# Four experts instead of three in 64-slot fp32 steps, and a new order of the 32 expert steps

## The reference

```
def moe_ffn(x, w_router, wg, wu, wd):
    B, S, D = x.shape
    xt = x.reshape(B * S, D)
    logits = (xt @ w_router).astype(jnp.float32)
    top_v, top_i = lax.top_k(logits, TOP_K)
    w = jax.nn.softmax(top_v, axis=-1)
    gates = jnp.sum(jax.nn.one_hot(top_i, N_EXPERTS, dtype=jnp.float32) * w[..., None], axis=1)
    y = jnp.zeros_like(xt)
    for e in range(N_EXPERTS):
        y = y + gates[:, e:e + 1].astype(xt.dtype) * swiglu(xt, wg[e], wu[e], wd[e])
    return y.reshape(B, S, D)
```

## Time and profile before

| | |
|---|---|
| median of 3 runs | 1435.05 us (1435.01 to 1440.6) |
| the profiled execution's own time | 1436.74 us |
| its span, from the first to the last instruction | 1435.0 us |
| TensorE busy, share of the span | 97% |
| VectorE, ScalarE busy | 57%, 49% |
| weights and other data moved | 444.37 MB |
| mean granted TensorE clock | 0.986 of full |

### The profile page before, as it was taken

One profiled execution on the slowest core, in us unless ns is written; L12 is line 12 of the kernel. 1 busy time (PEld: TensorE's weight loads), 2 busy tenths in 40 slices (PEclk: granted clock), 3 DMA queues, 4 the chain that ended last, 5 costly groups with the idle time before them and its releaser, 6 DMA issues.

```text
span 1435.0 us, 16626 instructions
## 1 busy us (share of the span) xinstructions
PE 1386.2 (97%) x6594; PEld 1001.5 (70%) x6594; DVE 818.8 (57%) x797; ACT 705.0 (49%) x768; POOL 36.9 (3%) x96
## 2 busy tenths in 40 slices
PE   7999999999899999999999999999999999999996
PEld 6875788888777747764657766767667757666575
DVE  4643545444455348573556666667547856547477
ACT  5552443444255436462356546455536546436364
POOL 2000000000000000000000000000000000000001
PEclk9999999999999899999999999999999999999999
DMA  9730855565344268999999999999999999999994
GB/s 337 243 118 1 297 201 176 178 201 173 122 152 136 100 263 297 336 407 402 391 411 404 405 373 405 409 410 409 405 399 411 410 409 402 409 410 409 402 403 159
DMA packets 148622, 444.37 MB, mean 310 GB/s; under 512 B 9470, under 2 KB 21628, under 8 KB 148540
## 3 DMA queue, kind: packets, MB, share of 16 engines
q1 hardware_dynamic: 146980, 438.24, 80.3%
q0 software_dynamic: 1440, 4.98, 0.9%
q10 hardware_dynamic: 120, 0.04, 0.0%
HBM read 439.30 MB, written 3.93 MB: 309 GB/s over the span
## 4 chain that ended last, share of the span: by engine, by line
PE 86%; DVE 5%; ACT 4%; DMA 2%; issue 2%; POOL 0%; DVEq 0%; POOLq 0%; SPq 0%; ACTq 0%
PE bank L835 83%; PE bank L838 3%; ACT part_h L1479 2%; DVE ring_l L1872 1%; DMA most<-in_moe_w_down_dram 1%; DMA ring<-in_moe_w_down_dram 1%; DVE most_l L1872 1%; DVE more_l L1872 0%; ACT xh L1479 0%; ACT prob L1663 0%; DVE y L1872 0%; ACT xn L1479 0%; DVE part_l L1872 0%; ACT probT L1479 0%; ACT in_h L1479 0%
## 5 line engine op out<-in xcount | busy, mean ns | idle before, releaser
L1479 ACT ACTIVATE part_h<-ring 128x2048 fp32r<-128x2048 f32 x142 | 270.2, 1917 | 135.0 <-PE bank L835 130.1
L835 PE MATMUL bank<-part_h,xh 128*128 128x512 f32 x784 | 311.1, 397 | 4.0 <-DVE xl L2182 1.3
L835 PE MATMUL bank<-part_h,xl 128*128 128x512 f32 x784 | 305.8, 390 | 0.0
L1872 DVE TENSOR_TENSOR ring_l<-ring,part_h 128x2048 fp32r<-128x2048 f32 x100 | 227.3, 2289 | 48.6 <-ACT part_h L1479 48.0
L835 PEld LDWEIGHTS bank<-part_h,xh 128*128 128x128 f32 x784 | 147.2, 188 | 43.7 <-issue 5.6
L835 PE MATMUL bank<-part_h,hTh 128*128 128x512 f32 x392 | 157.5, 402 | 19.0 <-DVE ring_l L1872 9.9
L835 PEld LDWEIGHTS bank<-part_h,xl 128*128 128x128 f32 x784 | 147.2, 188 | 31.5
L835 PE MATMUL bank<-part_h,hTl 128*128 128x512 f32 x392 | 154.6, 394 | 0.0
L1872 DVE TENSOR_TENSOR part_l<-part_in,part_h 128x2048 fp32r<-128x2048 f32 x57 | 129.9, 2289 | 33.0 <-ACT part_h L1479 32.5
L1872 DVE TENSOR_TENSOR part_l<-ring,part_h 128x2048 fp32r<-128x2048 f32 x42 | 96.1, 2292 | 84.1 <-ACT part_h L1479 84.1
L835 PE MATMUL bank<-part_l,xh 128*128 128x512 f32 x360 | 140.2, 389 | 0.0
(11 more groups left out here) (331 smaller groups left out, 1805.1 us busy)
## 6 DMA issues: line engine op xcount, KB each, us to landing
ring<-in_moe_w_down_dram SPq DMA_DIRECT2D x60, 1024.0 KB, 13.7
ring<-in_moe_w_up_dram SPq DMA_DIRECT2D x58, 1024.0 KB, 14.2
ring<-in_moe_w_gate_dram SPq DMA_DIRECT2D x50, 1024.0 KB, 10.1
part_in<-in_moe_w_down_dram SPq DMA_DIRECT2D x36, 1024.0 KB, 11.7
most<-in_moe_w_gate_dram SPq DMA_DIRECT2D x27, 1024.0 KB, 14.6
part_in<-in_moe_w_up_dram SPq DMA_DIRECT2D x27, 1024.0 KB, 13.0
part_in<-in_moe_w_gate_dram SPq DMA_DIRECT2D x21, 1024.0 KB, 14.9
most<-in_moe_w_up_dram SPq DMA_DIRECT2D x17, 1024.0 KB, 11.9
```

Of the source, the lines that this page charges most:

```text
L835: return nc.tensor.matmul(o, lhsT, rhs, start=start, stop=stop)
L1479: return nc.scalar.activation(dst, src, ACT.Copy, scale=scale)
L1872: return nc.vector.tensor_tensor(o, a, b, op)
```

## The change

Place 3 becomes narrow too, so four places of eight have 64 slots. The 32 steps are put in a new order, in which two narrow steps stand next to each other twice, at steps 10 and 11 and at steps 23 and 24. The places in the list at which rows are gathered (`GATHER_STEP`), slot lists are made (`SLOTS_AT`) and gates and rows for the fetches are worked out (`GATE_SHARES_AT`, `ROWS_KNOWN_AT`) move. The waits on TensorE for gathered rows are written so that they stand at the next wide step, since the next step may be narrow.

```diff
--- before.py
+++ after.py
@@ -74,7 +74,7 @@
     MC = len(MOE_CHUNKS)
     M = E * MC
     SLOTS, FEW = P, P // 2
-    NARROW = (False, True, False, False, True, False, True, False)
+    NARROW = (False, True, False, True, False, True, True, False)
     NARROWS = sum(NARROW)
     WIDE_AT = [a for a in range(E) if not NARROW[a]]
     NARROW_AT = [a for a in range(E) if NARROW[a]]
@@ -85,7 +85,7 @@
     wide_steps = [(a, c) for a in WIDE_AT for c in range(MC)]
     narrow_steps = [(a, c) for a in NARROW_AT for c in range(MC)]
     STEPS = [(narrow_steps if kind == "N" else wide_steps).pop(0)
-             for kind in "WWNWNWNW" "WNWNWWNW" "WNWNWWNW" "WNWNWNWW"]
+             for kind in "WWNWNWNW" "NWNNWNWN" "WNWNWNWN" "NWNWNWNW"]
     assert len(STEPS) == M and STEPS[0] == (0, 0) and STEPS[M - 1] == (E - 1, MC - 1)
     STEP_OF = {step: m for m, step in enumerate(STEPS)}
     STEP_CHUNK = [MOE_CHUNKS[c] for _, c in STEPS]
@@ -553,21 +553,22 @@
 
         TURN_AT = {turn_at(m, half): (m, half) for m in range(M)
                    for half in range(1 if STEP_NARROW[m] else halves(m))}
-        GATHER_STEP = {1: 1, 2: 4, 3: 6, 4: 9, 5: 14, 6: 19, 7: 22}
+        GATHER_STEP = {1: 1, 2: 4, 3: 8, 4: 13, 5: 15, 6: 23, 7: 24}
         GATHER_AT = {(last_piece(1, m) if e > 1 and NARROW[e] else MOE_AT[1, m, 1]): e for e, m in GATHER_STEP.items()}
-        SLOTS_AT = {MOE_AT[0, 1, 1]: 1, MOE_AT[0, 2, 3]: 2, last_piece(1, 4): 3, last_piece(1, 6): 4,
-                    MOE_AT[0, 11, 1]: 5, last_piece(1, 14): 6, MOE_AT[0, 20, 1]: 7}
+        SLOTS_AT = {MOE_AT[0, 1, 1]: 1, MOE_AT[0, 2, 3]: 2, last_piece(1, 4): 3, MOE_AT[0, 10, 1]: 4,
+                    last_piece(1, 13): 5, MOE_AT[0, 17, 1]: 6, MOE_AT[0, 24, 1]: 7}
         GATES_STEP = STEP_OF[NARROW_AT[-1], MC - 1]
         GATES_AT = MOE_AT[1, GATES_STEP, 0]
-        GATE_SHARES_AT = MOE_AT[1, 2, 1]
-        ROWS_KNOWN_AT = MOE_AT[1, 4, 1]
+        GATE_SHARES_AT = MOE_AT[0, 11, 1]
+        ROWS_KNOWN_AT = MOE_AT[0, 11, 3]
         for e, m in GATHER_STEP.items():
             assert m < STEP_OF[e, 0] and (e == 1 or STEP_NARROW[m])
             if e > 2 and not NARROW[e]:
                 assert STEP_OF[WIDE_AT[WIDE_AT.index(e) - 2], MC - 1] < m
             if e > 1 and NARROW[e]:
                 assert STEP_OF[NARROW_AT[NARROW_AT.index(e) - 1], MC - 1] <= m
-        assert not any(STEP_NARROW[m] and STEP_NARROW[m + 1] for m in range(M - 1))
+        WIDE_BEFORE = [max([i for i in range(m) if not STEP_NARROW[i]], default=0) for m in range(M)]
+        assert not STEP_NARROW[GATES_STEP + 1]
 
         def gather_bank(e, r):
 
@@ -1412,7 +1413,7 @@
                         if chunk == 0 and m:
                             pe.wait_ge(m_xl, rounds_before(e + 1, low=True))
                         for g, at in GATHER_STEP.items():
-                            if g > 1 and at == m - 1:
+                            if g > 1 and WIDE_BEFORE[m] < at < m:
                                 if NARROW[g]:
                                     pe.wait_ge(m_xe, rounds_before(g + 1))
                                 else:
```

## The result

| | before | after |
|---|---|---|
| median, first comparison (4 runs each) | 1435.03 us | 1458.95 us (1444.15 to 1459.68) |
| ratio | | 1.0106, 95% [1.0062, 1.0151] |
| median, second comparison (23 and 6 runs) | 1439.94 us (1433.63 to 1452.17) | 1455.2 us (1450.07 to 1458.5) |
| ratio | | 1.0112, 95% [1.0069, 1.0154] |
| span of the profiled execution | 1435.0 us | 1457.6 us; second 1450.8 us |

The change makes the kernel about 1.1% slower, some 16 us. The executions of one and the same kernel lie 15 to 19 us apart, so the ratio, which is formed from all of them, says more than a difference of two medians.

The account below looks back on a forecast made before the run. The prediction took the weight loads to set the pace: T at 1404.8, then store, fetch, queued VectorE work, the last two pieces and a 14.5 us tail summed to 1447.9, put at 1448 us, range 1441 to 1457.

Parts of the forecast that it names:

- the way home of the last narrow place's rows: Store, fetch and addition of step 30's output rows, forecast to stand bare behind the last weights; 1448 us, chance 0.67.
- T: Landing of the last weight load, 1412.0 us before the change; forecast to fall by 7.2 to 1404.8.
- 39 us less TensorE work: 42 pieces in four more narrow steps, each 0.94 us shorter on TensorE; hidden by the loads, counted as zero.
- slots and the smaller store: Weight stream: late-freed slots give back 2 us (bounds 0 and 3), place 3's smaller store 0.7 us.
- fetches leave the stream: The four row fetches come behind the weights, not among them; takes 4.5 us off T, bounds 4 and 6.
- store issue to fetch issue: From the store of the last narrow step's rows to the first fetch's issue; 5.6 us, bounds 3.4 and 6.6.
- fetch issue to the addition: From the first fetch's issue to its rows' landing, for which VectorE's addition waits; 6.3 us, bounds 2.6 and 8.7.
- last two pieces: Pieces 334 and 335 on TensorE after the wait for `hTl`; 5.8 us plus 2.1 us for the lower clock.
- tail: The rest, from TensorE's last pieces to the end (scatter, norm, store); 14.5 us as before.
- The row chain costs nothing in step 11: VectorE's row chain could stall TensorE some 4.5 us, but two narrow steps needing no split lie over it: zero.
- The rival with the short chain: Same chain behind T, but store and fetch take 3.4 and 2.6 us on idle DMA engines; 1442 us, chance 0.12.
- at 1412 or later: Sign that the forecast is wrong: the last weights landing at 1412 us or later, instead of about 1405.

Follow-up runs that it names:

- two wide steps last: The changed kernel with steps 29 and 30 exchanged, so the last narrow step is 29 and two wide ones follow; 1438.19 us, ratio to before 0.9999.
- new end alone: The kernel before, three narrow places, with steps 29 and 30 exchanged so that the last narrow step is 30; 1462.69 us, ratio 1.0161.
- the padded one: The kernel with two wide steps last, plus 60 small memsets on VectorE, one behind each of pieces 100 to 159; 1436.07 us, ratio 0.9951.

## Why the prediction was right, point by point

The sign and the mechanism were right: the way home of the last narrow place's rows stands bare behind T, VectorE waits for it with the last split and `hTl` queued behind (9.99 us), TensorE is idle (none busy from 1420.0 to 1432.8). The forecast was 1448 with 1441 to 1457; the two medians were 1458.95 and 1455.2, the first 2 us beyond the range, and the ratios, on the 1435.05 that it started from, give 1450 to 1451. That 1450 lies so near 1448 is in part luck: the parts of the change are +9.3 to +11.4 us where +12.9 was forecast, and the rest of the measured 16 us isn't in the sum at all. By its terms:

| term | predicted | measured |
|---|---|---|
| 39 us less TensorE work | 0 | 0: DMA share 1.03 in both |
| slots and the smaller store | -2.7 | -3.6 (before to two wide steps last), -4.7 (new end alone to after) |
| fetches leave the stream | -4.5 | -3.8 and -4.9 |
| T, from a mark in the stage | -7.2 | -8.5, twice |
| T to store issue | 4.7 | 4.1 |
| store issue to fetch issue | 5.6 | 3.3 |
| fetch issue to the addition | 6.3 | 4.5 |
| addition, split, `hTl` | 4.1 | 4.2 |
| last two pieces | 7.9 | 7.9 |
| tail | 14.5 | 16.9 |
| T to the end | 43.1 | 40.8 |

The measured times are those of the first profile of after. The store and fetch, 4.1 us too long, and the tail, 2.4 us too short, cancel for the greater part.

- **What bounds the kernel**, the loads: right. ScalarE lost 82 us of work in 610:1385 and VectorE 96, and the DMA share stayed 1.03.
- **The row chain costs nothing in step 11**: right, and with three narrow places it is a gain, since step 4 was a bad place for it (-2.9 us). With this the reason given for the slots is wrong in part: the two slow stretches of the earlier trace rows were put down to a run of wide work, but the same wide work runs at 400 instead of 385 GB/s once the chain is moved. Less the 0.7 us for the store, the slots measure 2.9 us by the one pair of kernels and 4.0 by the other, against 2 with bounds 0 and 3.
- **Store and fetch** are the terms that were mis-sized. I placed them near the rows of their own queue, taken under load. Measured without load they are 3.3 and 4.45 us, the first at the lower bound of 3.4 that I had worked out from the output's store. The rival with the short chain had this part right, 3.4, and was too short with 2.6 for the fetch. By the Trainium skill, "DMA: Bandwidth & Descriptors", section "Anatomy of one DMA, SWDGE (gpsimd) path" (2.0 us and the bytes at 436 GB/s, hence 2.3 and 3.2 us by estimate), the store agrees nearly: 2.53 us in the chain. The fetch of 0.5 MB does not, 4.45. On idle engines the rule is nearer than what I took for the store, and 1.2 us short for the gather.
- **The tail** was taken to be 14.5 as before. It is 16.9, from the long hole at one jump, a term that the forecast didn't have, since the rows before had the jump only where it was cheap.
- **The last weights** land at 1416.8 in the first profile, and "at 1412 or later" was named as a sign of being wrong. In the second profile it is 1407.9. Counted from piece 32 T falls by 8.5 us in both, so the sign was badly chosen: T counted from the start holds the clock of the attention too.
- **The other signs** came out: a wait of 9.99 us at the first addition, TensorE idle for 13.4 us (1419.5 to 1432.87), the store 4.1 us behind T, the lower clock at the last two pieces.
- **The start** was taken to be the same in both. The code is, the time is not: the profiled execution that I compared with had 10.2 us at the lower level in the attention, and others have up to 37.5 us. Most of the 11 us between the forecast and the first median is this: the profiled execution reached piece 32 13.3 us later, and the parts of the change were 3.6 us less than forecast.

The two parts that the change moves sum to +9.3 and +11.4 us. The fastest executions say the same, 1444.15 against 1433.63, and so do the slowest, 1459.7 against 1452.2 (10.5 and 7.5 us). The ratio says 16 us. The rest I take to be how often an execution fell into the group with the lowest clock: 6 of 10 after, and 6 of 7 with the new end alone, against 8, 8 and 14 of 23 for the kernel before in the three later comparisons. Whether the long wait at the end makes that group likelier, or this is chance with so few executions, stays open. Two things speak against TensorE's idle time as the cause. With TensorE kept busy in the wait (idle for 2.1 us instead of 13.4), the four executions are all at 1454 to 1459, and the profiled one had 34.1 us of the lower level in the attention. And the profiled executions of two kernels without a long wait at the end (two wide steps last, and the padded one) had 37.5 us of it.

What the change was worth without its end: two wide steps last bring 3.6 us in the stream, 1.2 us less from T to TensorE's last product, and lose 2.4 us at the jump. With the jump moved the parts are 4.4 us below before, and the fastest executions 3.9 us (1429.76 against 1433.63); the ratio of 0.9951, 7 us, holds the many executions near 1449 in its comparison too. Moving the row chain alone brings nearly as much, 4.1 us. So the room was some 4 us, and the order of the last steps costs 12 to 14 (+9.3 and +11.4 against -2.3).

## What to carry to other kernels

When work is moved at the end of a kernel, follow what leaves the engine through DRAM and comes back: the order of the last steps decides whether a store and a gather (here 4 + 3.3 + 4.5 us) lie under the last loads or behind them, and whatever stands in a list behind the instruction that waits for them pays as well. Cost a transfer by the load it will meet, not by the load under which its row was taken. And compare kernels from a mark inside the changed stage as well as by their whole time: the executions of one kernel lay 15 to 19 us apart here, as much as the change moved, and in the profiled ones the difference ahead of the mark went with a clock that fell in an untouched stage.

## What the runs showed of the hardware

- **A jump can cost 0.5 or 2.9 us**, by where it lies in the engine's list: 0.51 us in the three kernels with three narrow places, 2.8 to 2.9 in six with four, and 0.51 again with 60 instructions more ahead of it. Two packets of the instruction queues move near it in long and short cases alike, so what the long hole waits for isn't shown. The Trainium skill, "Advanced Engine Details and Errata", section "Control Flow Timing", has 51 ns for a branch and 108 ns for a compare and branch. Both holes here are longer; its section "ISA Cache" says that an engine holds only two lines of 256 instructions, which would fit a price that depends on the place; no run here shows what is held.
- **The same transfers on idle and on full queues.** Store of output rows to the next issue 3.3 us against 6.6, gather of rows 4.45 us against 8.7; the fourth of four gathers in flight 5.3 us in the kernel after, and 5.7 to 7.28 us in four other profiled executions, on otherwise idle engines.
- **The lower clock level differs between executions** in a stage of small matmuls and short waits: 3.4 to 37.5 us of it in the attention of layer 1, in unchanged code (37.5 and 13.7 in two executions of the kernel after). The executions of the kernel before lie in three groups from 1434 to 1452 us.
